# The last expert's rows added by selection products, one branch around the overflow loop, and seven weight pieces held behind the first gathers, in a decoder layer on Trainium2

## The reference

```python
top_v, top_i = lax.top_k(logits, TOP_K)
top_w = jax.nn.softmax(top_v, axis=-1)
g = jnp.minimum(xblk @ w_gate[e] + b_gate[e], 7.0)
u = jnp.clip(xblk @ w_up[e] + b_up[e], -7.0, 7.0)
y_e = ((u + 1.0) * g * jax.nn.sigmoid(1.702 * g)) @ w_down[e] + b_down[e]
x = x + g2 * sum_over_the_4_experts(top_w * y_e)
out = rms_norm(x, final_g)
```

## Time and profile before

| what | value |
|---|---|
| three runs | 1330.03, 1331.99, 1334.34 us, median 1331.99 |
| the profiled execution's own time | 1334.82 us |
| its span, first to last instruction | 1333.0 us |
| busy PE, DVE, ACT, POOL | 1251.9, 284.1, 193.0, 118.8 us |
| mean granted TensorE clock | 0.967 |
| mean DMA rate | 365 GB/s |

### The profile page before, as it was taken

How to read it: one execution, slowest core, us unless ns; L and a number is a source line. 1 busy time by engine, 2 the same in 40 slices (tenths; PEclk the granted TensorE clock), 3 DMA queues, 4 the chain that set the end, 5 groups by cost and what they waited for, 6 DMA issues and landing times.

```text
span 1333.0 us, 18761 instructions
## 1 busy us (share of the span) xinstructions
PE 1251.9 (94%) x7974; PEld 551.4 (41%) x7974; DVE 284.1 (21%) x562; ACT 193.0 (14%) x331; POOL 118.8 (9%) x178
## 2 busy tenths in 40 slices
PE   5889979959999999999999999999999999999976
PEld 2758847723333333333333333333333333333322
DVE  2643874673010000010000000001010010001027
ACT  3515251210000000000000000000001001000021
POOL 2011042010100000000001000000000001000000
PEclk9989979959999999999999999999999999999978
DMA  9647278399999999999999999999999999999973
GB/s 362 188 130 254 95 280 272 152 398 386 359 422 421 420 421 422 409 408 410 417 410 420 421 415 420 421 420 394 415 422 419 422 421 421 421 422 421 421 293 151
DMA packets 92004, 486.42 MB, mean 365 GB/s; under 512 B 13649, under 2 KB 21852, under 8 KB 41206
## 3 DMA queue, kind: packets, MB, share of 16 engines
q1 hardware_dynamic: 82451, 462.04, 86.3%
q0 software_dynamic: 8608, 20.82, 4.2%
q10 hardware_dynamic: 859, 2.32, 0.4%
HBM read 470.26 MB, written 18.04 MB: 366 GB/s over the span
## 4 chain that ended last, share of the span: by engine, by line
PE 81%; DMA 8%; DVE 5%; SPq 3%; ACT 1%; issue 1%; POOL 1%; ACTq 0%; DVEq 0%; POOLq 0%
PE psum L1941 61%; DMA raw<-in_moe_w_down 4%; PE psum L1593 4%; PE psum L1588 2%; PE psum L1589 2%; PE psum L1590 2%; SPq L518 2%; PE psum L1931 2%; PE psum L1760 1%; DMA cvs<-in_conv_dw 1%; PE psum L1656 1%; PE psum L2062 1%; DMA raw<-in_ada_w 1%; PE psum L1935 1%; POOL w_lo L687 1%
## 5 line engine op out<-in xcount | busy, mean ns | idle before, releaser
L1941 PE MATMUL psum<-raw,aT 128*64 128x512 f32 (+1 forms) x1728 | 301.2, 533 | 5.1 <-DMA raw<-in_moe_w_down 5.0
L1941 PE MATMUL psum<-raw,xb 128*64 128x512 f32 (+1 forms) x1920 | 304.6, 514 | 0.0
L1941 PE MATMUL psum<-raw,xa 128*64 128x512 f32 x1280 | 283.5, 595 | 0.0
L1514 DVE TENSOR_SCALAR act_t<-psum 128x512 f32<-128x512 f32 (+1 forms) x46 | 28.4, 642 | 874.7 <-PE psum L1941 874.7
L1941 PEld LDWEIGHTS psum<-raw,xb 128*64 128x64 f32 (+1 forms) x1920 | 100.6, 126 | 189.1 <-issue 176.7
L1941 PEld LDWEIGHTS psum<-raw,aT 128*64 128x64 f32 (+1 forms) x1728 | 98.3, 129 | 188.9 <-issue 166.7
L1941 PEld LDWEIGHTS psum<-raw,xa 128*64 128x64 f32 x1280 | 88.2, 137 | 169.7 <-issue 169.4
L701 POOL DMA_INDIRECT xrow<-h_scratch,gidx x24 | 27.4, 1143 | 464.1 <-PE psum L1593 430.0
L999 ACT ACTIVATE glu<-psum 128x512 f32<-128x512 f32 (+1 forms) x46 | 24.3, 559 | 291.8 <-PE psum L1941 291.8
L1588 PE MATMUL psum<-hT_hi,w_hi 128*128 128x260 f32 x208 | 59.4, 285 | 0.0
L1589 PE MATMUL psum<-hT_lo,w_hi 128*128 128x260 f32 x208 | 58.9, 283 | 0.0
(11 more groups left out here) (403 smaller groups left out, 912.6 us busy)
## 6 DMA issues: line engine op xcount, KB each, us to landing
raw<-in_moe_w_gate SPq DMA_DIRECT2D x128, 1024.0 KB, 26.2
raw<-in_moe_w_up SPq DMA_DIRECT2D x128, 1024.0 KB, 26.4
raw<-in_moe_w_down SPq DMA_DIRECT2D x128, 1024.0 KB, 27.1
raw<-in_ada_w SPq DMA_DIRECT2D x24, 1024.0 KB, 7.6
raw<-in_w_in SPq DMA_DIRECT2D x7, 1024.0 KB, 12.4
x<-in_x_prompt SPq DMA_DIRECT2D x2, 2048.0 KB
raw<-in_w_out SPq DMA_DIRECT2D x4, 1024.0 KB, 12.8
yrow_a<-y_scratch SPq DMA_DIRECT2D x2, 2048.0 KB, 10.6
```

The source lines that it names most:

```text
L1514: v.tensor_scalar(act_t[:, b, 0:bank.shape[1]], bank, 8.0, -6.0, ALU.min, ALU.max).then_inc(u_done, 1)
L1941: last = mm(out[w * g4:w * g4 + w, :], x, weights[:, 8 * w * g4:8 * w * g4 + 8 * w], start=start, stop=stop)
```

## The change

It has three parts. **Selection products.** The last expert's 64 rows are no longer scattered and fetched again. A block of zeros is scattered to their places early, and every tile adds those rows by a product with a selection matrix (`pick`) that holds a row's routing weight where the row belongs; the same product adds the down biases, because 32 of its rows are the turned routing weights and 32 rows of `last_y` are the biases. The fetch of the other results no longer waits for the last expert. The samples are laid out as four column groups on 128 partitions. `BY_PE` becomes 1, 2, 2, 3 for the four prompt tiles; the samples go to PE altogether. **Overflow.** Each engine has one branch around the whole loop, and on PE, ACT and POOL the loop stands before the last expert's down product. **Hold.** Pieces 11 to 17 also wait until the first two gathers have landed.

```diff
-BY_PE = (0, 2, 2, 3, 3)
+BY_PE = (1, 2, 2, 3)
+SENT = ALL_BLOCKS - 1
-EARLY, MIDDLE = 3, 15
+EARLY, HELD, MIDDLE = 3, 11, 15
...
         def extras(eng, cycle):
             n = eng.value_load(task_i[0:1, N_AT:N_AT + 1], min_val=0, max_val=XTRA)
-            with eng.Fori(0, XTRA // 8) as q:
-                with eng.If(q * 8 < n):
-                    with eng.Fori(q * 8, q * 8 + 8) as more:
-                        with eng.If(more < n):
-                            cycle(more)
+            with eng.If(n > 0):
+                with eng.Fori(0, XTRA) as more:
+                    with eng.If(more < n):
+                        cycle(more)
...
                 else:
                     sp.wait_ge(m_used, n - NBUF + 1)
+                if HELD <= n < NBUF:
+                    sp.wait_ge(x_rows[0], 16)
+                    sp.wait_ge(x_rows[1], 16)
                 m_load(n % NBUF, src)
...
-            sp.wait_ge(m_used, 372)
-            sp.dma_start(bdn[:, :], moe_b_down[0]).then_inc(bdn_loaded, 16)
+            sp.wait_ge(m_used, n * 12 + 374)
+            sp.dma_start(last_y[64:64 + E, 0, :], moe_b_down[0, :, 0:512]).then_inc(bdn_loaded, 16)
+            sp.dma_start(last_y[32:32 + E, 1, :], moe_b_down[0, :, 512:D]).then_inc(bdn_loaded, 16)
...
+            sp.wait_ge(zero_rows, 16)
             for b in range(5):
                 sp.wait_ge(y_out[b], n * 16 + 16 * y_uses(b) if b in X_BUFS else 16 * y_uses(b))
-            for i, t in enumerate(TAIL):
-                sp.dma_start(yrow[i][0:ROWS[t], :, :],
-                             y_d.rearrange("(p t j h) d -> p t j (h d)", t=TT, j=K, h=2)[0:ROWS[t], t, :, :])\
-                    .then_inc(fetched[i], 16)
+            sp.dma_start(yrow_s[:, :, :], rows_y[0:NB, TT - 1, :, :]).then_inc(fetched[TT - 1], 16)
+            for t in range(TT - 1):
+                if t == 1:
+                    sp.wait_ge(picked, 1)
+                    for g4 in range(4):
+                        q = slice(32 * g4, 32 * g4 + NB)
+                        for dst, src, c in ((x2s, x2_d[SEQ:TOK], 256 * g4), (g2s, mod_d[0:NB], 3 * D + 256 * g4)):
+                            sp.dma_start(dst[q, :], src[:, c:c + 256]).then_inc(e_loaded, 16)
+                if t == 2:
+                    sp.wait_ge(at_ps, ALL_BLOCKS)
+                if t == 3:
+                    sp.wait_ge(m_used, n * 12 + (12 * E - 3))
+                sp.dma_start(yrow[t], rows_y[:, t, :, :]).then_inc(fetched[t], 16)
...
         @block.gpsimd
...
             link(g.memset(xrow[:, :, :], 0.0))
+            link(g.memset(zero_y[:, :], 0.0))
...
             g.wait_ge(units_done, 1)
+            at_last = unit_of(ORDER[E - 1])
+            rows_to(y_d, sunit[:, at_last // 2, at_last % 2:at_last % 2 + 1], y_last, zero_y[:, :], zero_rows)
...
-            scatter(E - 1)
...
         @block.scalar
...
+            n = extras(act, extra)
+            act.wait_ge(WT_ps, 1)
+            for q, h in ((slice(64, 64 + E), 0), (slice(32, 32 + E), 1)):
+                ac.activation(pick[q, h, 0:4, :].rearrange("p a b -> p (a b)"), bk[0][0:E, :], ACT.Copy)
+                ac.activation(pick[q, h, 4, :], bk[1][0:E, 0:P], ACT.Copy).then_inc(WT_done, 1)
...
+            act.wait_ge(m_used, n * 12 + 12 * E)
+            ac.activation(last_y[0:64, 0, :], down_bank(E - 1, 0)[0:64, :], ACT.Copy).then_inc(y_a, 1)
...
         @block.vector
...
+            dve.wait_ge(WT_ps, 2)
+            for h in range(2):
+                q = slice(64 * h, 64 * h + 64)
+                for t in range(TT):
+                    weight = bk[4][q, P * t:P * t + P] if t < 4 else bk[5][q, 0:P]
+                    last = v.scalar_tensor_tensor(pick[q, h, t, :], iota1[q, :], keys[q, t:t + 1], weight,
+                                                  ALU.is_equal, ALU.mult)
+            dve.wait_ge(m_used, n * 12 + 12 * E)
+            v.tensor_copy(last_y[64:P, 1, :], down_bank(E - 1, 0)[64:P, :]).then_inc(y_a, 1)
...
+            combine_samples()
+            combine(0)
+            finish_samples()
+            for t in range(1, TT - 1):
+                combine(t)
+                finish(t - 1)
+            finish(TT - 2)
...
         @block.tensor
...
+            n = extras(pe, extra)
             for t in range(TT):
                 out = bk[0][0:E, t * P:t * P + P] if t < 4 else bk[1][0:E, 0:P]
                 last = turn(out, wfull[:, t, :], P)
             last.then_inc(WT_ps, 1)
+            def last_weights():
+                pe.wait_ge(WT_done, 2)
+                pe.wait_ge(picked, 1)
+                mm(bk[4], hot_e[64:96, :], pick[64:96, 0, 0:4, :].rearrange("p a b -> p (a b)"), start=True, stop=True)
+                mm(bk[5][:, 0:P], hot_e[64:96, :], pick[64:96, 0, 4, :], start=True, stop=True).then_inc(WT_ps, 1)
-            down([down_bank(E - 1, 0)], (64,), c0, full_at(c0))
+            down([down_bank(E - 1, 0)], (64,), c0, full_at(c0), 2, last_weights)
...
+            for g4 in range(4):
+                h, c = g4 // 2, 256 * (g4 % 2)
+                mm(bk[6][32 * g4:32 * g4 + 32, 0:256], pick[deep[h], h, TT - 1, 0:32], last_y[deep[h], h, c:c + 256],
+                   start=True, stop=False)
+            pe.wait_ge(fetched[TT - 1], 16)
+            for j in range(K):
+                for g4 in range(4):
+                    last = mm(bk[6][32 * g4:32 * g4 + 32, 0:256], diag_s[:, j, :], yrow_s[:, j, 256 * g4:256 * g4 + 256],
+                              start=False, stop=(j == K - 1))
+            for t in range(TT - 1):
+                if t == 3:
+                    pe.wait_ge(sde_done, 2)
+                for h in range(2):
+                    mm(bk[2 * t + h], pick[deep[h], h, t, :], last_y[deep[h], h, :], start=True, stop=False)
+                pe.wait_ge(fetched[t], 16)
+                for h in range(2):
+                    for j in range(BY_PE[t]):
+                        last = mm(bk[2 * t + h], diag[:, t, j, :], yrow[t][:, j, 512 * h:512 * h + 512],
+                                  start=False, stop=(j == BY_PE[t] - 1))
+                if t == 0:
+                    pe.wait_ge(sde_done, 1)
+                    mm(bk[6][:, 256:257], same[:, :], cols[:, SSQ:SSQ + 1], start=True, stop=True).then_inc(yb_ps, 1)
```

More of the change, by code:

```diff
@@ new lines, in _ @@
+            act.wait_ge(yb_ps, 3)
+            ac.activation(cols[:, RSTD:RSTD + 1], bk[6][:, 256:257], ACT.Sqrt, scale=1.0 / D,
+                          bias=cols[:, EPS:EPS + 1]).then_inc(sde_done, 1)
+            for t in range(TT - 1):
+                c1 = SSQ + 1 + t
+                act.wait_ge(acc_done, t + 2)
+                link(ac.activation(sq_e[:, :], acc[:, t % 2, :], ACT.Square, accum_out=cols[:, c1:c1 + 1]))
+                ac.activation(cols[:, RSTD + 1 + t:RSTD + 2 + t], cols[:, c1:c1 + 1], ACT.Sqrt,
+                              scale=1.0 / D, bias=cols[:, EPS:EPS + 1]).then_inc(sde_done, 1)
@@ new lines, in _ @@
+            v.tensor_scalar(hot_e[64:96, :], ones[64:96, :], hot_col[64:96, 0:1], None, ALU.mult).then_inc(picked, 1)
+            v.tensor_copy(same[:, :].rearrange("p (a b) -> p a b", a=4), id4[:, :].unsqueeze(1).to_broadcast([P, 4, 32]))
+            at_last = unit_of(ORDER[E - 1])
+            src = slice(64 * (at_last % 2), 64 * (at_last % 2) + 64)
+            for h in range(2):
+                link(v.tensor_copy(hot_col[64 * h:64 * h + 64, 1:2], gidx[src, at_last // 2:at_last // 2 + 1]))
@@ new lines, in combine @@
+            def combine(t):
+                A = acc[:, t % 2, :]
+                dve.wait_ge(fetched[t], 16)
+                dve.wait_ge(yb_ps, t + 3 if t else 2)
+                if t >= 2:
+                    dve.wait_ge(out_ready, t)
+                j = BY_PE[t]
+                link(v.scalar_tensor_tensor(two(A), two(yrow[t][:, j, :]), wts[:, t, j:j + 1],
+                                            psum[:, 2 * t:2 * t + 2, :], ALU.mult, ALU.add))
+                for j in range(BY_PE[t] + 1, K):
+                    link(v.scalar_tensor_tensor(A, yrow[t][:, j, :], wts[:, t, j:j + 1], A, ALU.mult, ALU.add))
+                link(v.tensor_tensor(A, A, g2b[:, :], ALU.mult))
+                v.tensor_tensor(A, A, x2e[:, t, :], ALU.add).then_inc(acc_done, 1)
@@ L1958, in project, with down @@
                     last.then_inc(m_used, 1)
-            def down(outs, widths, slot0, full):
+            def down(outs, widths, slot0, full, at_=0, between=None):
                 for j in range(4):
                     slot = (slot0 + j) % NBUF
+                    if j == 1 and between:
+                        between()
                     pe.wait_ge(m_full[slot], full(j))
@@ L1970, in down @@
                                 if w == size:
-                                    last = products(out, w, aT[:, b, k % n, w * (k // n):w * (k // n) + w],
+                                    last = products(out, w, aT[:, at_ + b, k % n, w * (k // n):w * (k // n) + w],
```

(40 more changed lines are left out.)

200 lines of the change are left out of this document (89 added, 111 removed).

## The result

The changed kernel takes **1323.59 us** (three runs, 1322.72 to 1324.71) against 1331.99 before: a ratio of 0.9936, 95% interval 0.9914 to 0.9958. The forecast was 1320.2 in a range of 1313.0 to 1327.5. The profiled execution took 1324.71 us, its span is 1322.9.

The account below looks back on a forecast made before the run. Weight stream, PE's stand with its slow clock, and DVE's final cycles bound the kernel. Tile 0 ready at 1290.7 plus 31.5, less 1.0 for the hold, ends at 1321.2, 11.8 less; 1331.99 - 11.8 = 1320.2 us, range 1313.0 to 1327.5.

Parts of the forecast that it names:

- rival A: The forecast itself: hold, moved PE branch and earlier DVE chain give 1320.2 us, bounds 1316 to 1325; chance 0.58.
- DVE's chain: From tile 0's first combine to the end: cycles of 8.4, 6.66, 6.66 and 9.84, together 31.5 us.
- the forecast's own signs of being wrong: Short PE branch, clock still at 0.5 at 1290, DVE waiting for a fetch, or DVE's cycles growing.
- C: After PE's stand the clock stays down 19.8 us from the restart, costing 9.9 instead of 2.5: 1327.6 us; chance 0.08.
- D: PE's clock stays down through the whole tail, so PE runs late and DVE waits: 1347.1 us; chance 0.07.
- E: Weights under way keep gathers at 8.9 us, PE starts no earlier, pieces come 2.5 later: 1323.7 us; chance 0.12.
- Part 1, the hold: At the first gathers: stream pause loses 1.8 to 2.5 us, dents at 320 to 350 return 2.85; last piece 1.0 earlier.
- Part 2, the branch: PE's single branch before the last down: load of n at 1265.5, jump 5.4 us from 1266.7, PE resumes at 1272.1.
- Rival B: The jump is cheap at its new place, down ends at 1277.1, then tile 0's fetch binds: 1314 us; chance 0.15.
- The clock: After PE's stand before the last down: 5 us at half speed, 2.5 us lost, bounds 1.7 and 9.9.
- the forecast's PE sum: PE after the branch: last down ends 1284.2, copies 1284.8, samples 1287.2, tile 0's products 1290.7.
- Part 3: The tail: tile 0's fetch takes 8.4 us, landing 1282.4 or up to 3 later, hidden by PE at 1287.

Follow-up runs that it names:

- e2: Changed kernel with PE's usual case (no overflow) falling straight into the tail, a second tail copy behind the loop: 1323.77 us, 0.9944 of the kernel before.
- e1: Changed kernel without the hold on pieces 11 to 17: 1326.14 us, 0.9958 of the kernel before.
- e3: Changed kernel with x2 and both gains loaded behind tile 0's fetch, the samples' eight small loads ahead of it: 1324.88 us, 0.9956 of the kernel before.
- e5: Changed kernel with the hold starting at piece 8 instead of 11: 1326.69 us, 0.9969 of the kernel before.
- e4: Changed kernel with both the fall-through PE branch and x2 and gains loaded behind tile 0's fetch: 1325.25 us, 0.9955 of the kernel before.
- e6: Changed kernel with the fall-through PE branch and x2 and gain loads spread between the four tile fetches: 1319.74 and, repeated, 1318.00 us.
- e9: Changed kernel with fall-through PE branch and loads spread between the tile fetches, but without the hold: 1321.78 us, 0.9932 of the kernel before.

## Why the prediction was right, point by point

**Direction and range: right; the path through tile 0 in part.** What bounds the kernel was read rightly, and most of rival A, the forecast's own mechanism, is what happened: PE stands at the new place, the last down follows it, and DVE's chain starts earlier by more than it grows. But tile 0's data were to be there before PE came to them; in the profile the fetch ended last, just behind PE. Two of the forecast's own signs of being wrong came up: the first combine hung on a fetch, and the clock stood at half until 1290, though by a second fall and not, as in C or D, by staying down. It came out 3.4 us above the forecast. That this is E's 1323.7 is chance: E loses its 3.5 us at the last piece, and of the miss only 0.9 lies there. Which part gave what is shown only in part: the hold most likely 1 to 2 us, the branch alone some 2 by its traces. The rest, some 4 to 5 of the 8.4, falls to the selection products and the branch's new place by subtraction; no run has the selection products alone.

**Part 1, the hold: right in size, wrong in how.** Worth 1.0 by the forecast, 0 in the first pair of profiles, 1 to 2 over all. The pause cost 3.2 us by the share, where the forecast had 1.8 to 2.5 (the 1.8 came from no row). "With pieces 11 to 17 behind, PE may start up to 2.7 us earlier" failed: the gather came only 0.4 sooner (1.2 by the means over all profiles, 8.0 against 9.2), as the pieces already under way kept it slow. So the dents filled with hardly any of the earlier start of PE that was to fill them, and between 295 and 350 SP waits for PE to free buffers as long as before (46.5 against 46.7 us). What moved is the lost share, from 320 to 350 to 280 to 290: the held pieces come later and are still to be moved when SP waits. That this is why DMA has work there is likely; no run tests it by itself. Rival E was right on the gather and wrong on its price of 2.5, which the dents give back.

**Part 2, the branch: right.** The load of n came at 1262.6; with the 1.8 us of the early part that is 1264.4, one microsecond before the forecast's 1265.5. The jump took 6.24 us instead of 5.4, so PE resumed at 1271.6 on the forecast's scale, against 1272.1. A row shows 6,244 ns where the branch jumps over the loop and 89 ns where it falls through (e2). The Trainium skill's page Advanced Engine Details and Errata, Control Flow Timing, gives some 108 ns for a compare-and-branch: the row that falls through is near it, the jump over the body is far above. The Trainium skill's page Runtime: NRT & Kernel Launch, Instruction fetch mechanics, says that a taken branch to a target not held must fetch it first: the trace agrees. By the room that this section gives PE the jump would have been free, as the prediction had weighed; the 6,244 ns decide against that. The DMA queues of the changed kernel during the jump, 1263.48 to 1269.72 (packets, MB, share), have one transfer of 16 KB on the instruction queue q8:
```profile
q8 instruction: 1, 0.02, 1.2%
```
It starts 3.6 us after the jump does and takes 1.2, and the jump ends 1.5 us behind it. Each of the fourteen long jumps of these profiles has one such transfer inside it, and behind the branches of 86 to 89 ns none comes on that queue for 5 us. What fills the time before the transfer no run shows.

**Rival B, the cheap jump.** e2 made the jump cheap and 1314 did not come. Its step "the fetch binds then: 1282.4" had the same fault as the forecast: the fetch landed behind the loads.

**The clock: first fall right, second missed.** After the stand half speed lasted 3.4 us, worth 1.7 instead of 2.5, the lower bound. The second fall, 6.8 us over tile 0's products, was in no term; with it half speed cost some 5 us of PE's work. Both lengths vary: over the five profiles with the stand (changed kernel twice, e1, e3, e5) the first lasts 3.4 to 6.8 us, the second 3.4 to 10.2. e3, where the fetch is out of the way, prices the slip: 17.7 us from last piece to combine where the forecast's PE sum gives 15.6.

**Part 3: the term that was mis-sized.** "The shortest fetch of 2 MB took 8.4: 1282.4, or up to 3 later behind the x2 loads" took 15.28 (the 1273.6 and 8.4 add up to 1282.0, not 1282.4, which changes nothing). I had noted that x2 and the gains start later, and asked whether they would be late themselves; that they are 3.1 MB ahead of the fetch on the same queue I priced at 3 us instead of 7.5. In the kernel before, the wait for the last scatter hid them: its fetches were issued from 1284.1 on, behind a stretch in which DMA stood nearly idle (a share of 0.08 from 1280 to 1284). "That is hidden by PE at 1287" therefore fell: PE and the fetch came within 0.4 us of each other (18.0 with both, 17.7 with the fetch out of the way). DVE's chain was right: 31.7 against 31.5.

**The sum of the miss**: 0.9 from the hold in that pair of profiles, 2.4 from tile 0 (fetch and clock, equal bounds), 0.2 from DVE's chain; 3.5, less 0.1 between profile and medians.

## What to carry to other kernels

When a wait is removed ahead of a transfer, add up the bytes that are queued in front of it and divide by the stream's rate: the wait may have hidden them. When a fix brings nothing, test it together with the next bound (here 89 ns for a branch and 7 us off a fetch, each worth nothing, together 8 us), and then look for the third. Holding back a stream that sets the pace moved its idle time here; it paid by what it filled of a later gap, and not by the earlier start of the engine behind it (e5).

## What the runs showed of the hardware

The taken jump over the same loop on PE took 5,379 to 6,672 ns at either place, with one branch or three, and 3,582 to 4,225 ns as the last thing PE did (e2, e4, e6, e9), where it also skips the second copy of the tail. In all fourteen the instruction transfer takes 0.9 to 1.2 us and the jump ends 1.4 to 1.6 us behind it; what differs is the time before it, 2.8 to 4.1 us ahead of the tail and 1.0 to 1.8 at the end. Where the kernel before takes the same jump a second and a third time, it costs 227 and 221 ns.

The first gather of 96 rows takes 4.50 us with no weights beside it (e5), 7.1 to 8.6 with the last pieces ahead of the hold, and 8.9 to 9.5 in the full stream.

The clock's second fall is not tied to the products. Two profiled executions of e6 run the same instructions at the same place; the stretch 1279 to 1283 in the first and in the second:
```profile
1279.00:1283.00 4.00, 4.00 (x16) 1.64 (x9) 0.85 (x2) 1.79 (x3) 0.00 (x0) 0.50 1.00 408
```
```profile
1279.00:1283.00 4.00, 3.74 (x36) 1.48 (x35) 0.85 (x2) 1.10 (x3) 0.00 (x0) 1.00 0.95 402
```
In both PE stood for 0.89 us for `last_y` shortly before; one went to 1.2 GHz and the other stayed at 2.4. They differ a little ahead of that: for the last down piece PE stood 0.87 us in the first and 0.50 in the second. I had not expected that, and no run here settles what decides it.
